# Gate projection by seven half-size block products a pair of chunks instead of eight, in a one-core Trainium2 block kernel

## What is computed

```
mod = jax.nn.silu(c) @ ada_w[l] + ada_b[l]
h = rms_norm(x, norm1_g[l]) * (1.0 + scale1) + shift1
p = h @ w_in[l]                      # h is 1024x1024
q, k, v, f_logit, p_rwkv, gate_logit = jnp.split(p, IN_SPLITS, axis=-1)
... token_shift(p_rwkv, mu) = p + (prev - p) * mu ...
g_fox, g_rwkv = jnp.split(jax.nn.sigmoid(gate_logit), 2, axis=-1)   # gate_logit is 1024x2048
merged = g_fox * (o_fox @ w_out_fox[l]) + g_rwkv * (o_rwkv @ w_out_rwkv[l])
```

## Time and profile before

| | us |
|---|---|
| median of 3 runs | 1745.97 |
| lowest, highest | 1743.08, 1756.0 |
| the profiled execution, its span | 1746.0 |
| PE busy | 1612.2 |
| PEld (weight loads) busy | 1177.4 |
| DVE busy | 749.2 |
| ACT busy | 464.4 |
| POOL busy | 354.3 |

### The profile page before, as it was taken

How to read it: one execution, slowest core, us unless ns; L and a number is a source line. 1 busy time by engine, 2 the same in 40 slices (tenths; PEclk the granted TensorE clock), 3 DMA queues, 4 the chain that set the end, 5 groups by cost and what they waited for, 6 DMA issues and landing times. The chain is left out here.

```text
span 1746.0 us, 33968 instructions
## 1 busy us (share of the span) xinstructions
PE 1612.2 (92%) x14322; PEld 1177.4 (67%) x14322; DVE 749.2 (43%) x1262; ACT 464.4 (27%) x899; POOL 354.3 (20%) x703
## 2 busy tenths in 40 slices
PE   5999999899998997798989999979999999999986
PEld 5688888878787884577777878846655555454442
DVE  5655455441104775688755446682111111111114
ACT  1642111121214774454542132221000000000002
POOL 1100011110002000667752011101222222121211
PEclk9999999999998998899998999999999999999998
DMA  9357765651225641232263514387999999999977
GB/s 337 134 194 277 258 209 188 211 173 68 74 87 123 153 129 41 62 75 51 53 187 118 191 50 157 124 357 282 392 404 422 422 423 422 422 423 418 402 318 300
DMA packets 144503, 398.57 MB, mean 228 GB/s; under 512 B 49027, under 2 KB 65462, under 8 KB 126944
## 3 DMA queue, kind: packets, MB, share of 16 engines
q1 hardware_dynamic: 114096, 328.77, 51.2%
q0 software_dynamic: 15504, 41.34, 6.6%
q10 hardware_dynamic: 14752, 26.29, 4.0%
HBM read 342.79 MB, written 64.17 MB: 233 GB/s over the span
## 5 line engine op out<-in xcount | busy, mean ns | idle before, releaser
L2938 PE MATMUL psum<-w,ex_x_t 128*64 128x256 f32 x1376 | 155.5, 381 | 7.0 <-DMA w<-in_exp_w 6.1
L2938 PEld LDWEIGHTS psum<-w,ex_x_t 128*64 128x64 f32 x1376 | 96.6, 137 | 59.5 <-DMA w<-in_exp_w 9.7
L167 PE MATMUL psum<-w_even,h_hi 128*128 128x512 f32 (+1 forms) x320 | 118.9, 372 | 7.3 <-ACT stage L567 7.3
L567 ACT ACTIVATE stage<-psum 128x512 f32<-128x512 f32 (+1 forms) x72 | 41.3, 574 | 302.5 <-PE psum L169 185.4
L169 PE MATMUL psum<-w_even,h_lo 128*128 128x512 f32 (+1 forms) x320 | 118.4, 370 | 0.0
L168 PE MATMUL psum<-w_even,h_hi 128*128 128x512 f32 (+1 forms) x320 | 118.3, 370 | 0.0
L3098 DVE TENSOR_TENSOR ex_sig_m<-psum,ex_sig_m 128x256 f32<-128x256 f32 x32 | 13.6, 425 | 239.8 <-ACT ex_sig_m L3062 239.8
L3062 ACT ACTIVATE ex_sig_m<-psum 128x256 f32<-128x256 f32 x32 | 12.3, 384 | 385.0 <-PE psum L2938 385.0
L167 PE MATMUL psum<-w_odd,h_hi 128*128 128x512 f32 x256 | 100.0, 391 | 0.0
L169 PE MATMUL psum<-w_odd,h_lo 128*128 128x512 f32 x256 | 99.6, 389 | 0.0
L168 PE MATMUL psum<-w_odd,h_hi 128*128 128x512 f32 x256 | 99.6, 389 | 0.0
(11 more groups left out here) (522 smaller groups left out, 3653.5 us busy)
## 6 DMA issues: line engine op xcount, KB each, us to landing
w<-in_exp_w SPq DMA_DIRECT2D x64, 2048.0 KB, 34.1
w_mixed<-in_exp_w SPq DMA_DIRECT2D x31, 2048.0 KB
w_ring<-in_ada_w SPq DMA_DIRECT2D x12, 2048.0 KB, 10.6
w_ring<-in_w_in SPq DMA_DIRECT2D x10, 2048.0 KB, 10.4
qk<-stage_r ACTq DMA_DIRECT2D x16, 512.0 KB, 7.4
gates<-stage ACTq DMA_DIRECT2D x32, 256.0 KB, 2.0
bl_gates<-gates SPq DMA_DIRECT2D x8, 1024.0 KB, 4.9
w<-pair_rows SPq DMA_DIRECT2D x16, 512.0 KB, 10.0
```

Of the source, the lines that this page charges most:

```text
L167: nc.tensor.matmul(out, a_hi, b_hi, start=(i == 0), stop=False)
L567: nc.scalar.activation(stage[:, b, 0:n], ps[:, 0:n], ACT.Sigmoid if kind == "gate" else ACT.Copy).then_inc(sig("proj_evac"), 1)
L2938: last = mm(ps[h * MAIN:(h + 1) * MAIN, j * FH:(j + 1) * FH], x_t[:, k, 0:MAIN], w[:, k, h * FH:(h + 1) * FH], start=(k == 0), stop=(k == ...
```

## The change

The four gate chunks are no longer chunks of the loop. They are two pairs of chunks, and a pair is one product of a 1024x1024 matrix with a 1024x1024 one, cut in 2x2 blocks A11, A12 (the first 512 tokens), A21, A22 (the rest) and B11 to B22. It is done by the Winograd form of Strassen's scheme: seven block products, here called windows w = 0 to 13 (seven a pair, i = w % 7), each of four rows r of 128 tokens by 512 columns with 12 matmuls (4 blocks of K, three products). The feature operands are A11, A12, S2, A22, S1, S3, S4 with S1 = A21 + A22, S2 = S1 - A11, S3 = A11 - A21, S4 = A12 - S2; the weight operands are B11, B21, T2, T4, T1, T3, B22 with T1 = B12 - B11, T2 = B22 - T1, T3 = B22 - B12, T4 = B21 - T2.

- **Feature sums** are made by DVE once, for both pairs (`feature_sum`, passes of 128x2048), ACT makes their high parts (`high_sum`), DVE the low ones (`rest`): S1 in chunk 5, S2 in chunk 6, S4 in windows 0 and 2, S3 behind the rows of windows 3 and 4.
- **Weight sums** are made by DVE in the ring, for each pair (`weight_sums`, `prepare`); each window's weights are split again in a high part (`high_unit`, ACT) and a low one (`prepare`, DVE), 128x2048 each. The loop of DVE over the windows puts `prepare(w + 1)` in front of the rows of window w.
- **The outcome of a window** is added to what is kept of the others: ACT copies the rows of window 0 out, DVE adds the rows of all the others from PSUM (`evict`), 28 additions a pair; the sigmoids are then taken from SBUF by ACT.
- **Modulation** moves forward: the accumulate of piece 11 from tile (4, 7) to (4, 3), the biases behind tile (4, 5), PE's sums in front of the tiles (4, 6) and (4, 7), each time waiting for all biases, ACT's copies to (4, 7) and (5, 0). S1 lies where `mod_bc` has its rows 0 to 3: these are stored to DRAM (`mods`, 16 KB) before S1 is made and spread from there over the partitions (2 MB) by SP in `attend`, in front of the loads of `qk_odd`.
- **Stage places**: the narrow tiles have six places of 256 columns instead of three (`stage_place`, `stage_before`).
- **The ring**: the gate weights come in quarters of 1 MB (`load_raw`).

The memset of `qk_even` stands in window 12, and there are 116 semaphores for a stage instead of 100.

```diff
+PAIRS_OF = D // NC5
+PRODUCTS = 7
+HK = KT // 2
...
+RAW_SLOT = ({"11": 2, "21": 3, "12": 0, "22": 1}, {"11": 3, "21": 2, "12": 0, "22": 1})
+RAW_ORDER = ("11", "21", "12", "22")
+UNIT_OF = ("11", "21", None, "21", "11", "12", "22")
+SUMS_AT = {(4, 6): range(0, 4), (4, 7): range(4, 8)}
+SUMS_OUT_AT = {(4, 7): range(0, 4), (5, 0): range(4, 8)}
 MOD_BEHIND = {1: (4,), 2: (5, 6), 3: (7, 8, 9), 4: (10,), 5: (11,)}
-MOD_AT = {(0, 7): 4, (1, 4): 5, (1, 7): 6, (2, 3): 7, (2, 5): 8, (2, 7): 9, (3, 7): 10, (4, 7): 11}
+MOD_AT = {(0, 7): 4, (1, 4): 5, (1, 7): 6, (2, 3): 7, (2, 5): 8, (2, 7): 9, (3, 7): 10, (4, 3): 11}
...
-        self.proj += [("gate", j, w_in[:, :, COL_G + j * NC5:COL_G + (j + 1) * NC5]) for j in range(2 * D // NC5)]
+        self.gate = lambda p, role: w_in[:, (int(role[0]) - 1) * HK:int(role[0]) * HK, COL_G + (2 * p + int(role[1]) - 1) * NC5:COL_G + (2 * p + int(role[1])) * NC5]
...
+    def load_raw(self, sp, p, role):
+        sp.dma_start(self.raw(p, role), self.gate(p, role)).then_inc(self.sig(f"raw_{role}_in"), 16)
...
+        NARROW = len(proj) - 1
...
+        OPERAND = (a11, a12, s2, a22, s1, s3, s4)
+        WINDOWS = PAIRS_OF * PRODUCTS
...
+        def stage_place(m):
+            b, n = (V_TILES + m) % 3, rwkv_part(m)[2]
+            lo = (m - WIDE_TILES) // 3 % 2 * n if m >= WIDE_TILES else 0
+            return stage[:, b, lo:lo + n]
+        def stage_before(m):
+            return m - 3 if m < WIDE_TILES + 3 else m - 3 * (2 if m >= WIDE_TILES + 6 else 1 + (m >= WIDE_TILES + 3))
...
-            weights.load(sp, range(CHUNKS, len(weights.order) - 2))
-            sp.wait_ge(sig("proj_full"), V_TILES + 16 + RWKV_TILES)
-            weights.load(sp, range(len(weights.order) - 2, len(weights.order)))
-            sp.wait_ge(sig("ring_used"), len(weights.order))
+            weights.load(sp, range(CHUNKS, len(weights.order)))
+            for role in RAW_ORDER:
+                sp.wait_ge(sig("ring_used"), len(weights.order) - (1 if role[1] == "1" else 0))
+                weights.load_raw(sp, 0, role)
+            sp.wait_ge(sig("a2_ready"), 1)
+            sp.dma_start(dram["mods"][0:1, :], mod_bc[0:1, 0:4, :].rearrange("p a n -> p (a n)")).then_inc(sig("mods_out"), 16)
+            for p in range(1, PAIRS_OF):
+                for i, role in enumerate(RAW_ORDER):
+                    sp.wait_ge(sig("u_lo"), PRODUCTS * (p - 1) + 4 + i)
+                    weights.load_raw(sp, p, role)
+            sp.wait_ge(sig("u_lo"), WINDOWS)
...
+            def prepare(w):
+                p, i = w // PRODUCTS, w % PRODUCTS
+                (hi, lo), total = unit[w % 2], unit_sum[w % 2]
+                q = {role: weights.raw(p, role) for role in RAW_ORDER}
+                if i == 2:
+                    dve.wait_ge(sig("prod"), 4 * (w - 1))
+                    weights.raw_arrived(dve, p, "22")
+                    dve.wait_ge(sig("t1_sum"), p + 1)
+                    tt(total, q["22"], q["11"], ALU.subtract).then_inc(sig("t2_sum"), 1)
+                    dve.wait_ge(sig("t2_sum"), p + 1)
+                    tt(q["21"], q["21"], total, ALU.subtract).then_inc(sig("t4_sum"), 1)
+                    dve.wait_ge(sig("u_hi"), w + 1)
+                    tt(lo, total, f32(hi), ALU.subtract).then_inc(sig("u_lo"), 1)
+                else:
+                    dve.wait_ge(sig("u_hi"), w + 1)
+                    tt(lo, q[UNIT_OF[i]], f32(hi), ALU.subtract).then_inc(sig("u_lo"), 1)
+            def weight_sums(p):
+                q = {role: weights.raw(p, role) for role in RAW_ORDER}
+                dve.wait_ge(sig("u_lo"), PRODUCTS * p + 1)
+                weights.raw_arrived(dve, p, "12")
+                tt(q["11"], q["12"], q["11"], ALU.subtract).then_inc(sig("t1_sum"), 1)
+                weights.raw_arrived(dve, p, "22")
+                tt(q["12"], q["22"], q["12"], ALU.subtract).then_inc(sig("t3_sum"), 1)
+            def feature_sum(name, total, *terms):
+                x = terms[0][1]
+                for op, y in terms[1:]:
+                    n = feature_steps[name] = feature_steps.get(name, 0) + 1
+                    tt(total, x, y, op).then_inc(sig(f"{name}_sum"), 1)
+                    dve.wait_ge(sig(f"{name}_sum"), n)
+                    x = total
+            def rest(s, total, name):
+                dve.wait_ge(sig(f"{name}_hi"), 1)
+                tt(s[1], total, f32(s[0]), ALU.subtract).then_inc(sig(f"{name}_lo"), 1)
...
+            def evict(p, i, r):
...
+                    tt(out_buf[b], u2[:, r, :], product, ALU.add).then_inc(sig("c11_sum"), 1)
+                elif i == 2:
+                    tt(u2[:, r, :], u2[:, r, :], product, ALU.add).then_inc(sig("u2_sum"), 1)
...
+                    if (j, i) == (4, 5):
+                        dve.wait_ge(sig("bias_in"), 16 * 8)
+                        for m in range(4, 12):
+                            row, place = bias_place(m)
+                            tt(mod_dst(m)[row, :], mod_dst(m)[row, :], f_work[row, place, :], ALU.add).then_inc(sig("mod_biased"), 1)
+                    if (j, i) == (5, 1):
+                        dve.wait_ge(sig("g2_in"), 16)
+                        dve.wait_ge(sig("bc_evac"), 8)
+                        stt(out=mod_bc[:, 2, :], in0=mod_bc[:, 2, :], scalar=1.0, in1=mod_bc[:, 4, :],
+                            op0=ALU.add, op1=ALU.mult).then_inc(sig("a2_ready"), 1)
+                    if (j, i) == (5, 3):
+                        dve.wait_ge(sig("mods_out"), 16)
+                        feature_sum("s1", s1_sum, (ADD, f32(a21[0])), (ADD, f32(a21[1])), (ADD, f32(a22[0])), (ADD, f32(a22[1])))
+                    if (j, i) == (5, 5):
+                        prepare(0)
+                    if (j, i) == (NARROW, 0):
+                        dve.wait_ge(sig("proj_full"), 8 * NARROW)
+                        feature_sum("s2", s2_sum, (ADD, s1_sum), (SUB, f32(a11[0])), (SUB, f32(a11[1])))
+                        rest(s1, s1_sum, "s1")
+                    if (j, i) == (NARROW, 3):
+                        weight_sums(0)
+                    if (j, i) == (NARROW, 5):
+                        rest(s2, s2_sum, "s2")
+            for w in range(WINDOWS):
+                p, i = w // PRODUCTS, w % PRODUCTS
+                if w == 0:
+                    shift(RWKV_TILES - 1)
+                if w + 1 < WINDOWS:
+                    prepare(w + 1)
+                if i == 0 and p >= 1:
+                    weight_sums(p)
+                if w == 0:
+                    feature_sum("s4", s4_sum, (ADD, f32(a12[0])), (SUB, f32(s2[0])), (ADD, f32(a12[1])))
+                if w == 12:
+                    nc.vector.memset(keep["qk_even"][HD:KB, 2, :, :].bitcast(F32), 1.0).then_inc(sig("q_ones"), 1)
+                for r in range(4):
+                    evict(p, i, r)
+                if w == 2:
+                    feature_sum("s4", s4_sum, (SUB, s4_sum), (SUB, f32(s2[1])))
+                    rest(s4, s4_sum, "s4")
+                if w == 3:
+                    feature_sum("s3", s3_sum, (ADD, f32(a11[1])), (SUB, f32(a21[1])), (ADD, f32(a11[0])))
+                if w == 4:
+                    feature_sum("s3", s3_sum, (SUB, s3_sum), (SUB, f32(a21[0])))
+                    rest(s3, s3_sum, "s3")
...
+            def high_unit(w):
+                p, i = w // PRODUCTS, w % PRODUCTS
+                hi = unit[w % 2][0]
+                if i == 2:
+                    act.wait_ge(sig("t2_sum"), p + 1)
+                    src = unit_sum[w % 2]
+                else:
+                    role = UNIT_OF[i]
+                    src = weights.raw(p, role)
+                    weights.raw_arrived(act, p, role)
+                    if i in (3, 4, 5):
+                        act.wait_ge(sig(("t4_sum", "t1_sum", "t3_sum")[i - 3]), p + 1)
+                    if w >= 2:
+                        act.wait_ge(sig("prod"), 4 * (w - 1))
+                    else:
+                        act.wait_ge(sig("proj_full"), 8 * (NARROW - 1 + 2 * w))
+                nc.scalar.activation(hi, src, ACT.Copy).then_inc(sig("u_hi"), 1)
...
+            def high_sum(s, total, name, steps):
+                act.wait_ge(sig(f"{name}_sum"), steps)
+                nc.scalar.activation(s[0], total, ACT.Copy).then_inc(sig(f"{name}_hi"), 1)
...
+                    for m in SUMS_OUT_AT.get((j, i), ()):
+                        act.wait_ge(sig("bc_full"), m + 1)
+                        nc.scalar.activation(mod_dst(4 + m), bc_bank(m), ACT.Copy).then_inc(sig("bc_evac"), 1)
...
+                        if earlier >= 0:
+                            act.wait_ge(sig("shift_sum"), earlier + 1)
...
+                    if (j, i) == (5, 4):
+                        high_sum(s1, s1_sum, "s1", 3)
+                        high_unit(0)
+                    if (j, i) == (NARROW, 3):
+                        high_sum(s2, s2_sum, "s2", 2)
...
-                if j == SUM_BEFORE:
-                    pe.wait_ge(sig("mod_biased"), 8)
```

(30 more changed lines are left out.)

175 lines of the change are left out of this document (142 added, 33 removed).

## The result

The changed kernel takes 1785.33 us (median of 4 runs, 1778.28 to 1791.13), the kernel before beside it 1746.45 (4 runs, 1743.08 to 1756.0). The ratio is 1.0204, 95% interval 1.0152 to 1.0255: slower by 2%, or 39 us. The forecast was 1772 and slower by 26, with a range up to 1784. The sign is right, and the time lies 1.3 us above the range.

A forecast was written before the change was run, and what follows sets the result against it. PE, busy except for narrow-chunk waits, bounds the kernel. Saving 31.6 us against waits of 21.8, 2.1, 19.9 and 7.7, three clock echoes of 1.6, plus 0.75 and 0.5, gives +26: 1772 us, 8-in-10 range 1753 to 1784.

The forecast's parts named there:

- What is taken away: Gates and narrow chunk: 96 of 768 matmuls go (21.8 us), six narrow places end waits (9.8), together -31.6 us.
- The first wait: Before tile (4, 6) PE waits 21.8 us for DVE's biases; 2.1 more for ACT's copy before (4, 7).
- The second wait: Before window 1 PE waits 19.9 us for B21's low part, behind `shift(31)` in DVE's list; bounds 12.5 and 26.
- The third wait: Before window 5 PE waits 7.7 us for S3's last pass, high part and low part, behind window 4's fourth row.
- The echo of the clock: After each of the three long waits PE runs at 1.2 GHz for a while, charged 1.6 us each.
- What hides: In all other windows DVE's and ACT's chain stays under the window's 10.9 us; window 2 is covered by 1 us.
- The end over DVE and ACT: End of `front`: the last rows go over DVE and ACT instead of ACT alone, +0.75 us.
- The reload: In `attend`, 2 MB in front of `qk_odd` make its loads late: 0 to 3 us, taken as 0.5.
- Behind front nothing else changes: After `front`, apart from the charges of 0.75 and 0.5 us, the stages were to stay the same.
- the rival at 1782: POOL's issues on the shift chain wait out DVE's 2.28 us passes, four or five times: +10 us, chance 0.09.
- The chain didn't catch up: Rival: the shift chain catches up while PE stands at (4, 6), removing the second wait: -21.5, 1751 us, chance 0.13.
- Faster: Rival: biases are ready when PE reaches (4, 6) and the shift chain isn't behind: 1727 us, chance 0.08.

The follow-up runs named there:

- spread: The changed kernel with the same work in another order on DVE's and ACT's lists and PE's sums before (5, 4) and (5, 5): 1728.52 us, ratio 0.9874.
- places3: The changed kernel with three stage places for the narrow tiles instead of six: 1781.82 us, ratio 1.0184.
- b_sums: The kernel before with only the modulation's accumulate, biases, sums and copies moved forward: 1761.94 us, ratio 1.0102.
- b_semaphores: The kernel before with only the declarations added, 116 semaphores instead of 100 and the unused DRAM tensor `mods`: 1747.66 us, ratio 0.999.
- b_mods: The kernel before with only the store of `mods` and its 2 MB reload in `attend` added: 1749.23 us, ratio 1.0.
- spread_early: As spread, but with PE's sums back in front of tiles (4, 6) and (4, 7), ACT's copies following: 1751.13 us, ratio 1.0012.
- late: The changed kernel with PE's sums in front of (5, 2) and (5, 3), ACT's copies, a2, S1 and S2 moved back: 1757.94 us, ratio 1.0061.
- prep1: The changed kernel with DVE making the low part for window 1 behind tile (6, 4), in front of the last shifts: 1788.92 us, ratio 1.0261.

## Why the prediction was right, and where it fell short

**What is taken away: right.** The 96 matmuls and the narrow chunk's waits are worth 31.6 us by the prediction. spread, in which nothing queues, has a `front` 29.9 us shorter than before, with 0.9 us of waiting left. The narrow chunk took 23.03 us for the forecast 23.3. But a second execution of before has a `front` of 450.3, with 2.4 us less of waits in this chunk, so the 9.8 us are the price of one execution. And they were put down to the six places: in after these do shorten the narrow chunk (23.0 us for 28.8 in places3), but nothing of it reaches the end, and in b_sums three places did as well. The duration of 0.2267 us a matmul was the right one. By the Trainium skill, page "TensorE: Matmul & The Clock Gate", section "Back-to-back issue gap", with its 131 ns for 512 columns, the 96 matmuls would have brought 12.6 us instead of 21.8, 9.2 less; the length of spread's `front` bears out the 0.2267 of the trace.

**The first wait: right.** Forecast DVE done at 291.4, PE's first sum was at 292.81; PE came to the wait at 271.89 instead of 269.7, since all of `front` begins 2.5 us later in this execution. The waits are 20.5 and 1.8 us for the forecast 21.8 and 2.1.

**The second wait: right in its mechanism, its place and its size.** 18.9 us for the forecast 19.9; `shift(31)` started at 407.03, where the forecast has it end at 408.2, and the low part ended at 410.57 for 410.5. It lies inside the bounds of 12.5 and 26.

**The third wait: right.** 7.4 for 7.7.

**The echo of the clock: under-sized by 1.3 us.** Three times 1.6 were charged. Behind the second and the third wait PE ran for 4.6 and 5.5 us at half the clock, which costs half of these, 2.3 and 2.7. Behind the first wait the first four sums were slower:

```profile
292.80:296.00 3.20, 3.19 (x4) 1.45 (x5) 1.20 (x2) 0.00 (x0) 0.00 (x0) 0.55 0.52 164
```

The next tile's first matmul started at 297.36, so the four sums took 4.55 us for the forecast 3.4: 1.1 lost. Together 6.1 for 4.8. In the sum of `front` this is more than made up for by waits that were each a little shorter than forecast, 2.9 us together. Some 1.5 us of `front` are in no term. That its sum came out at 24.6 for 24.7 is therefore partly luck.

**What hides: right.** No other window of after has a wait, window 2 with its cover of 1 us neither.

**The end over DVE and ACT: under-sized by 1.7 us.** 0.75 was charged, 2.4 was measured in after, and 2.1 to 2.6 in all kernels with the new end (hand-over 7.8 to 8.2 for 5.66). The last rows in after:

```profile
565.36 0.69 DVE L612 TENSOR_TENSOR u<-u,psum 128x512 f32<-128x512 f32 x1 [2.03 <-PE psum L191]
566.08 0.63 ACT L802 ACTIVATE u<-u 128x512 f32<-128x512 f32 x1 [2.09 <-DVE u L612]
566.74 0.33 ACTq L804 DMA_DIRECT2D gates<-u  x1
571.77 0.21 POOL L1098 MEMSET causal<- 128x128 f32 x1 [162.56 <-POOLq L95]
```

And in before:

```profile
538.34 0.60 ACT L567 ACTIVATE stage<-psum 128x512 f32<-128x512 f32 x1 [4.84 <-PE psum L169]
538.97 0.33 ACTq L573 DMA_DIRECT2D gates<-stage  x1
542.34 0.21 POOL L786 MEMSET causal<- 128x128 f32 x1 [159.94 <-POOLq L95]
```

The additional row is the forecast 0.75. The rest lies behind the last issue: from there to POOL's first instruction of `attend` it is 5.03 us for 3.37 before. The rows of these last stores in the view of DMA issues (KB, us to landing), 566.5 to 567 us of after, then 538.9 to 539.2 of before, show what it is:

```profile
gates<-u ACTq DMA_DIRECT2D x1, 256.0 KB, 3.6
gates<-stage ACTq DMA_DIRECT2D x1, 256.0 KB, 2.1
```

1.55 of the 1.66 us are the slower landing (3.60 for 2.05), and only 0.11 lie behind it, though the clearing of the stage's semaphores takes 0.64 us for 0.37. In b_semaphores, which declares 116 but uses no more than before, clearing and hand-over are as before. The stretches up to the last issue, after and before, show that the store goes into DMA engines that are full (the last two numbers are their busy share and GB/s):

```profile
555.00:567.00 12.00, 10.32 (x46) 8.22 (x44) 3.51 (x6) 5.06 (x8) 0.00 (x0) 1.00 1.04 333
526.00:539.00 13.00, 12.31 (x55) 9.86 (x53) 0.00 (x0) 1.79 (x3) 0.00 (x0) 1.00 0.11 40
```

In after the loads of q and k are issued from 547.93 to 555.85, right in front of the end, in before from 471.36 to 479.41, and after has more gate stores in these last microseconds. No run moves them, so this is read from the trace and not tested. The prediction looked at the engines at the end of the stage, and not at the store.

**The reload: not refuted.** 0.5 was charged. b_mods has none that can be measured, with an interval of 6.8 us to either side; `attend` is 1.0 us longer in after than in before, 0.6 in b_mods, but 1.1 in b_semaphores, which has no reload.

**"Behind front nothing else changes": the step that failed.** It holds for the instructions, as far as the profiles show. It doesn't hold for the time: 9 us in the mean over nine runs of eight kernels. The measured 39 against the forecast 26 are this term (10.9 in after), the end (1.7) and 0.5 of `attend` beyond the charge. No wait in `front` was overlooked, and it is none of the rivals. About half goes with a lower granted clock, by the estimate above; what brings it stays open. Without it the time would lie inside the range. The range's upper end came from the bounds of the second wait and the rival at 1782, and left no room for this, nor for the 13 us over which the three runs of before spread.

**The rivals.** The chain didn't catch up by window 1: `shift(31)` ended at 408.4, not by 388.3. In spread_early PE gets nothing of the first wait back; in b_sums it gets some 9 us back in the narrow chunk, where waits fall away. Nobody starved POOL: its issues take 0.55 us as before. Faster would have needed biases in time; late and spread, where PE asks for them only when they are there, show that this was the right condition, but late by itself gained only 24 us.

## What to carry to other kernels

- Saved matmuls become time only if the engine that prepares the operands keeps its list short in front of each of PE's waits. The same work, with as many instructions on DVE and PE, took 477.8 or 423.4 us of `front` here, by its order alone. Before moving work to a chain with round trips, write down DVE's list with its times; it told all three waits to within 1.3 us.
- Long passes belong one at a time into the gaps that a round trip leaves, and what PE reads next goes in front of what nobody reads soon. To take away one wait of several on one list hands it on (prep1); order the whole list.
- Price the end of a stage up to the last store that lands, and let the range take in the scatter that the runs before show, here 13 us among three. A single execution is no ground for a few us: `recur` of one and the same kernel differed by 12.

## What the hardware showed that was not expected

- The granted clock in the same stage with the same instructions was 0.91 in one execution of the kernel before and 0.87 in another, and `recur` took 367.4 or 379.8 us, with nothing else different that the profile shows.
- A wait of 18.9 us was followed by 4.6 us of work at 1.2 GHz, one of 7.4 us by 5.5 us: the shorter wait had the longer echo. The price of a wait here was its length and 1.1 to 2.7 us more.
- The last store of `front`, 256 KB, landed after 2.0 to 2.1 us in the five profiled executions without the block products, and after 3.3 to 3.8 in the nine with them. In after the DMA engines were busy all the time in front of it, in before for 0.11 of it.
